# Head norms of layers 2 and 3: square root and reciprocal in place of logarithm and exponential

## The reference

```python
# retention (layer 2), each of 12 heads
out = out * lax.rsqrt(jnp.mean(out * out, axis=-1, keepdims=True) + EPS)
# gated delta net (layer 3), each of 4 heads
q = q * lax.rsqrt(jnp.sum(q * q, axis=-1, keepdims=True) + EPS) * (DN_HEAD_DIM ** -0.5)
k = k * lax.rsqrt(jnp.sum(k * k, axis=-1, keepdims=True) + EPS)
# short convolution (layer 3), 8 groups of 64
y = rms_norm(y, norm_g.reshape(CONV_A_GROUPS, CONV_A_GROUP_DIM))
```

## Time and profile before

| | us |
|---|---|
| median of 3 runs | 1966.63 (1966.19 to 1968.82) |
| the profiled execution | 1973.07 |
| its span, first to last instruction | 1971.1 |
| mean granted PE clock | 0.959 |

### The profile page before, as it was taken

The page is one execution under the profiler, slowest core; times in us unless marked ns, Lnnn a source line. Parts: engine busy times, 40 slices in busy tenths (PEclk is TensorE's granted clock), DMA queues, the critical chain, the costliest instruction groups (busy, mean ns, idle before and its releaser), DMA issues.

```text
span 1971.1 us, 23226 instructions
## 1 busy us (share of the span) xinstructions
PE 1799.6 (91%) x9382; PEld 1274.0 (65%) x9382; DVE 939.3 (48%) x1564; ACT 606.6 (31%) x1073; POOL 79.8 (4%) x90
## 2 busy tenths in 40 slices
PE   5999999999988999999995889988957999999996
PEld 4978888888867877777763668778842333333332
DVE  4344555455564554544555565654661333333334
ACT  5433233333333323333244554423320111111102
POOL 0000000000000000000000000052011000000000
PEclk8999999999988999999996989989978999999999
DMA  5612222122312112222221122300276999999995
GB/s 197 214 65 86 86 75 97 69 92 97 118 43 96 65 65 97 75 95 77 75 78 40 43 86 86 107 1 12 118 304 256 420 420 420 420 420 420 420 421 242
DMA packets 50894, 326.17 MB, mean 165 GB/s; under 512 B 8224, under 2 KB 8272, under 8 KB 14176
## 3 DMA queue, kind: packets, MB, share of 16 engines
q1 hardware_dynamic: 44320, 305.65, 39.4%
q0 software_dynamic: 6320, 17.95, 2.7%
q10 hardware_dynamic: 144, 1.05, 0.1%
HBM read 323.50 MB, written 5.31 MB: 167 GB/s over the span
## 4 chain that ended last, share of the span: by engine, by line
PE 72%; DMA 11%; DVE 8%; ACT 5%; issue 3%; POOL 1%; SPq 0%; DVEq 0%; ACTq 0%; POOLq 0%
PE PJ L533 15%; PE PJ L535 15%; PE PJ L534 15%; PE PJ L2211 7%; DMA m_b<-in_w_moe 4%; DMA m_a<-in_w_moe 4%; PE PJ L2225 3%; PE PB L2237 2%; PE PB L1973 2%; DMA m_c<-in_w_moe 1%; PE PB L2038 1%; PE PB L1934 1%; PE PB L1966 1%; PE PB L2052 1%; DVE x L1357 1%
## 5 line engine op out<-in xcount | busy, mean ns | idle before, releaser
L533 PE MATMUL PJ<-hT_hi,w_hi 128*128 128x512 f32 x832 | 343.8, 413 | 7.5 <-DVE x L1357 6.1
L535 PE MATMUL PJ<-hT_hi,w_lo 128*128 128x512 f32 x832 | 327.0, 393 | 0.0
L1158 DVE TENSOR_TENSOR w_lo<-w_raw,w_hi 128x1024 fp32r<-128x1024 f32 (+1 forms) x224 | 228.2, 1031 | 207.3 <-ACT w_hi L752 207.0
L534 PE MATMUL PJ<-hT_lo,w_hi 128*128 128x512 f32 x832 | 326.8, 393 | 0.0
L752 ACT ACTIVATE w_hi<-w_raw 128x1024 fp32r<-128x1024 f32 (+1 forms) x224 | 196.1, 899 | 14.9 <-PE PJ L535 13.6
L533 PEld LDWEIGHTS PJ<-hT_hi,w_hi 128*128 128x128 f32 x832 | 158.1, 190 | 48.3 <-issue 16.1
L534 PEld LDWEIGHTS PJ<-hT_lo,w_hi 128*128 128x128 f32 x832 | 158.2, 190 | 36.8 <-issue 6.1
L535 PEld LDWEIGHTS PJ<-hT_hi,w_lo 128*128 128x128 f32 x832 | 157.6, 189 | 34.6
L808 ACT ACTIVATE sc<-sc,stats 128x256 f32<-128x256 f32 (+2 forms) x80 | 43.4, 542 | 326.1 <-DVE stats L1238 326.1
L1737 DVE TENSOR_TENSOR x<-x,PB 128x512 f32<-128x512 f32 x128 | 82.0, 683 | 113.0 <-PE PB L2237 112.9
L533 PE MATMUL PJ<-w_hi,oT_hi 128*128 128x512 f32 x256 | 109.6, 428 | 8.7 <-DVE oT_lo L1282 8.7
(11 more groups left out here) (386 smaller groups left out, 2712.5 us busy)
## 6 DMA issues: line engine op xcount, KB each, us to landing
w_raw<-in_w_all SPq DMA_DIRECT2D x92, 1024.0 KB, 4.8
m_b<-in_w_moe SPq DMA_DIRECT2D x88, 1024.0 KB, 26.9
m_a<-in_w_moe SPq DMA_DIRECT2D x71, 1024.0 KB, 26.6
m_c<-in_w_moe SPq DMA_DIRECT2D x22, 1024.0 KB, 27.1
m_d<-in_w_moe SPq DMA_DIRECT2D x11, 1024.0 KB
aux<-scr_c POOLq DMA_DIRECT2D x6, 512.0 KB, 4.6
aux<-in_decay POOLq DMA_DIRECT2D x6, 512.0 KB, 4.3
gbc<-in_gains POOLq DMA_DIRECT2D x4, 512.0 KB, 6.7
```

The lines of the kernel that those rows point to most:

```text
L533: pe.matmul(dst, lh, rh, start=start, stop=False)
L534: pe.matmul(dst, lh, rl, start=False, stop=False)
L535: return pe.matmul(dst, ll, rh, start=False, stop=stop)
L1158: dve.tensor_tensor(w_lo[:, n % SPLIT, j * w:(j + 1) * w], w_raw[:, n % RAW, j * w:(j + 1) * w], w_hi[:, n % SPLIT, j * w:(j + 1) * w].bit ...
```

## The change

In layer 2 ACT computes the square root of the mean square (with `EPS` as bias) instead of the logarithm and the exponential of minus half of it. DVE takes the reciprocal of this, 128x512, in place, before it multiplies. In layer 3 the same is done for the 8 norms of q and k and the 4 of the short convolution: ACT's second instruction and its link go, and DVE gets a reciprocal with a link in front of each multiplication. The norm of the delta net's output keeps logarithm and exponential. There are 24 norms in all, 12 in each layer. The whole diff:

```diff
--- before.py
+++ after.py
@@ -735,10 +735,9 @@
                 ins.then_inc(a_ch, 1)
                 act.wait_ge(a_ch, ch[0])
 
-            def rsqrt(dst, src, scale):
-
-                link(act.activation(dst, src, ACT.Ln, scale=scale, bias=epst))
-                return act.activation(dst, dst, ACT.Exp, scale=-0.5)
+            def root(dst, src, scale):
+
+                return act.activation(dst, src, ACT.Sqrt, scale=scale, bias=epst)
 
             def split_hi(n, j):
 
@@ -825,7 +824,7 @@
                     act.activation(sq[:], PO[:], ACT.Square).then_inc(o_act, 1)
                 if in_layer(k - 3, layer) and units[k - 3]["kind"] == "ret" and units[k - 3]["i"] == NT - 1:
                     act.wait_ge(ms_done, units[k - 3]["ret"] + 1)
-                    rsqrt(sq[:], PT[:], 1.0 / HD).then_inc(sd_done, 1)
+                    root(sq[:], PT[:], 1.0 / HD).then_inc(sd_done, 1)
 
             def evacuate(s):
                 st = steps[s]
@@ -912,10 +911,8 @@
                 rs_ = root_group(s)
                 for r in rs_:
                     act.wait_ge(q_sum, r + 1)
-                    link(act.activation(sq2[:, r % 4, :], PJ[norm_steps[r] % 2][:, S:2 * S], ACT.Ln,
-                                        scale=0.25 if r < 8 else 1.0 / 64, bias=epst))
-                for r in rs_:
-                    act.activation(sq2[:, r % 4, :], sq2[:, r % 4, :], ACT.Exp, scale=-0.5).then_inc(q_sd, 1)
+                    act.activation(sq2[:, r % 4, :], PJ[norm_steps[r] % 2][:, S:2 * S], ACT.Sqrt,
+                                   scale=0.25 if r < 8 else 1.0 / 64, bias=epst).then_inc(q_sd, 1)
 
             def decay_logs():
 
@@ -1285,6 +1282,7 @@
             def ret_scale(k):
                 un = units[k]
                 dve.wait_ge(sd_done, un["ret"] + 1)
+                link(dve.reciprocal(sq[:], sq[:]))
                 dve.tensor_tensor(og[:], og[:], sq[:], ALU.mult).then_inc(og_used, 1)
                 dve.wait_ge(og_used, un["ret"] + 1)
                 split_head(un)
@@ -1380,6 +1378,7 @@
             def finish_one(r):
                 q = sq2[:, r % 4, :]
                 dve.wait_ge(q_sd, r + 1)
+                link(dve.reciprocal(q, q))
                 if r < 8:
                     y = (gq, gk)[r // 4][:, r % 4, :]
                     dve.scalar_tensor_tensor(y, y, 0.5 * QK_SCALE if r < 4 else 0.5, q,
```

## The result

The changed kernel takes 2000.41 us (median of 4 runs, 1998.98 to 2002.13), the kernel before 1967.72 (4 runs, 1966.19 to 1970.04) beside it: a ratio of 1.0157 with a 95% interval of 1.0144 to 1.0169. By this ratio it is 30.9 us slower (28.3 to 33.3); the two medians by themselves are 32.7 apart. The forecast was 1994 us in a range from 1984 to 2010. The profiled execution took 2000.62 us, against 1973.07 of the one before, on which the sum was made: 27.6 us more, where the sum said 27.5. That agreement flatters the sum a little: in the trace after, the gate of the first changed place starts 1.85 us earlier than in the trace before, through stages that the change doesn't touch. From there on the added time is 17.0 us in layer 2, 12.0 in layer 3 up to 1272 us, and 0.5 behind it, 29.5 in all, which lies in the interval of the ratio.

A forecast was written before the change was run, and what follows sets the result against it. PE was taken to bound layer 2, ACT and DVE layer 3's column stage. Layer 2's 13.9, the clock's 3.4 and layer 3's 10.2 gave 27.5 us more: 2000.6 profiled, 1994 on the median, range 1984 to 2010.

The forecast's parts named there:

- rivals 1: All changed places: the reciprocal takes eight passes, 4.4 us each, giving 2020 us in all; chance 0.09.
- Rival 2: All changed places: a cheap reciprocal of some 0.5 us makes the kernel faster, 1953 us; chance 0.05.
- rival 4: Table loads don't fall because the table is changed back for Copy: +9 us, 2004 us in all; chance 0.04.
- (a): Layer 2, first head of a regular group, four times: the o step's addition ends 1.01 us later, 4.0 us in all.
- (b): Layer 2, fifth first head at 989.7 us: idle time covers the reciprocal, only the z evacuation touches PE, 0.1 us.
- (c): Layer 2, regular second heads, four times: the rotation behind the reciprocal comes 1.41 us later, 5.6 us in all.
- (d): Layer 2, last three heads: PE waits for the output split and the ending chain, 3 x 1.4 = 4.2 us.
- The clock: Layer 2: PE's clock drops behind two of four lengthened rotation pauses, 3.4 us; bounds 0 and 6.8.
- Layer 3, pairs: Four q/k pairs: two reciprocals lengthen the DVE and ACT chain, 2.4, 2.9, 2.4 and 2.5 us, 10.2 in all.
- The wait of the column sums: Layer 3, 1110 to 1165 us: PE's wait for ACT falls from 13.2 to about 5 us.
- Singles: Layer 3, four short-convolution norms: costed at nothing, covered by PE's two buffers; up to 2 us if that cover is gone.
- The page's price of a table switch: Skill's 2.66 us per switch, drain included, not adopted; it would make the sum about 15 us smaller.

The follow-up runs named there:

- e8: Kernel before with only layer 2's norms changed, four regular second heads finished on DVE behind the next group's second rotation: 1976.10 us, ratio 1.0030.
- e7: Kernel before with square root and reciprocal in layer 3 alone, products needing reciprocals moved to later steps, Exp table requested early: 1965.95 us, ratio 0.9985.
- e2: Kernel before with only layer 2's norms changed, layer 3's left as before: 1987.65 us, ratio 1.0082.
- e5: Changed kernel plus a one-column dummy Exp ahead of ACT's waits in decay_out: 1997.31 us, ratio 1.0147 to the kernel before.
- e4: Changed kernel without the reciprocals, ACT's Sqrt taken of a scaled sum, so the head norm is left out: 1950.94 us in one run.
- e1: Kernel before with only layer 3's norms changed, layer 2's left as before: 1984.69 us, ratio 1.0067.

## Why the prediction was right, and where it was off

- **The bound.** Right: free time on DVE in the mean was no cover, and what decided was the instruction directly behind each reciprocal. e8 and e7 show it: moved, the same instructions cost 10 us less in layer 2, and in layer 3 16 less, with the table load moved too.
- **The reciprocal, 3.35 us.** Right to 0.01 us: 3.346 and 3.350 measured. The slope between 1 and 16 elements holds to 512: (3350 - 252) / 496 = 6.25 ns an element against 6.3. With this rivals 1 (4.4 us) and 2 (0.5 us) fell, and so did eight passes as the reading of the repeat count of 8 that the Trainium skill gives in VectorE: DVE Perf Modes, section First, the fixed hardware budget: at 1.05 ns a pass these rows show six.
- **The root and the loads.** The root is 0.69 us as assumed. 25 loads are left in the changed places, where I had counted some 23; but 2 before the Tanh at L897 had stood there before and weren't among my 40, so 17 went, as forecast. None stands before a Copy, so rival 4 fell too (its +9 on 1994 makes 2003 us, not 2004). ACT's busy time fell by 37.7 us (forecast 37).
- **(a) First heads.** 1.01 forecast, 0.98 to 1.02 in the trace, four times; 0.43 of it comes already at the z evacuation, one step before the addition that the sum named. (b) 0.1 forecast, 0.08.
- **(c) Second heads.** 1.41 forecast, 1.43 to 1.45 where the clock held. (d) The last three: 1.4 forecast, 1.44 and 1.44 for the two that end the layer; the first of the three shows 2.65 us between 1005 and 1023 us, of which 1.44 is PE's longer pause (1.83 to 3.27) and 1.2 the clock behind it, which e2 doesn't have. The last one's shift of 1.4 had shrunk to nothing by 1087 us, in a stretch where the clock of the trace before was low.
- **The clock.** Two of four rotation places forecast at 1.7 us each; it fell at two, at 1.5 each. The count was luck: e2, with the same four pauses, has one. The forecast looked for the clock only behind new pauses; it also moved at two old ones, at the tenth head (+1.2) and behind the last (-1.4).
- **Layer 3, pairs.** Forecast 2.4, 2.9, 2.4 and 2.5; measured 2.37, 4.12, 2.38 and 3.15. Here the sum was 1.8 us short, 12.0 for 10.2. Of this 1.27 is the second pair's table load behind a wait (e5). The step that failed was the count of loads: I placed each new one where an old one had stood, and missed that a removed Exp had also been the one that fetched the table for an Exp further on. The fourth pair's 0.6 is the clock behind a pause of 6.60 us in front of PE's last sum, which the sum didn't look at: in e5, where the clock came back sooner, ACT's copy set the pace as forecast, and the pair cost 2.36 for 2.5.
- **The wait of the column sums.** Forecast to fall from 13.2 to about 5 us. The wait for the root fell to 3.1, but PE's wait as a whole rose to 19.0 (15.9 and 3.1), with the Square named. I had the chain right, in DVE and ACT, and didn't follow it one step further to PE, which stands behind it and waits for the same Square.
- **Rival 2.** It took a reciprocal of 0.5 us to be worth 13.5 us. e4, with none at all, was 20.7 shorter, 2.7 of them by the clock. At the last three heads the difference (4.3 against 5.8) is just those 0.5 us each; at the second heads (1.2 against 2.2) and in layer 3 (8.0 against 10.0) the rival was priced somewhat low.
- **Singles.** Nothing forecast; the copy of 1229.25 is 2.0 us later than the steps around it, as the sum had it, and the gates at 1255 us and behind stand where those of 1192.56 stood: nothing came through.
- **The page's price of a table switch.** The Trainium skill, ScalarE: Activation LUTs, section What ACT_TABLE_LOAD costs, has a drain of 1380 ns in a switch. These traces show a load of 1283 ns and the activation behind it 10 to 20 ns later (1163.46 + 1.28, then 1164.76), and the second heads lost 1.43 and not 0.03: the measurement decides against the drain here.
- **The median.** 2000.4 for 1994, for small reasons: 2.0 in the trace (29.5 for 27.5: 1.8 more in layer 3, 0.3 less in layer 2, 0.5 behind them), 1.1 between the medians of before in the two sets of runs (1967.72 and 1966.63), and the other 3.3 in the scatter of a few executions; the interval of the difference is 28 to 33 us, and the sum's 27.5 lies just below it.

## What to carry to other kernels

Before an operation is moved from one engine to another, look at what stands in the queue directly behind it on the new engine and who waits for that; half a free engine is no cover for 3.35 us in front of a result for which TensorE waits already, and in layer 2 the same instruction behind the next rotation was free. The reciprocal could be priced from the slope between two small shapes of the same kernel. When an activation is removed, look also for the next one that had used the table it had loaded: where the new load comes to stand behind a wait it is fully exposed, as at L929, and an activation of one column ahead of the wait hides it.

## What was not expected of the hardware

- A table load can stand ahead of the wait of its activation or behind it. From 700 us on, every load of the changed kernel but one starts 0.02 us behind the activation before it, and where its own activation has to wait it is hidden: that of the Tanh at 1131.11, behind which ACT waits 7.58 us, and those of the second heads' roots, behind which it waits 6.8. The one at L929 stands behind its wait: ACT was idle for 9.82 us and only then loaded for 1.28. With an activation of its own ahead of the wait it was hidden (e5). No run here shows what sets the order.
- Four pauses of the same 1.75 us before the same work: the granted clock stayed at 1.00 behind two of them and averaged 0.62 over 4.5 us behind the other two. Each execution shows it at other places. Layer 2 of e1 is that of before, yet e1 gains 2.3 us on it between 1035 and 1087 us; from 1048.3 to 1053.3 its clock was 1.00 and that of before 0.82 (e1 first, then before):

```profile
1048.30:1053.30 5.00, 5.00 (x24) 4.14 (x23) 3.13 (x4) 4.08 (x7) 0.00 (x0) 1.00 0.00 0
```

```profile
1048.30:1053.30 5.00, 5.00 (x20) 4.04 (x19) 3.13 (x3) 2.58 (x4) 0.00 (x0) 0.82 0.00 0
```

In the same 5 us e1 issued 24 matmuls and the kernel before 20. So one trace against another is uncertain by some 2 us in a layer, before any change.
